# An fp32 encoder layer on one core: the key transpose on VectorE, the scores' diagonal by a column sum, and other moves around TensorE

## What is computed

```python
forget = lb + (1.0 - lb) * jax.nn.sigmoid(ff)
k = (1.0 - lb) * jax.nn.sigmoid(-ff)
# per chunk, G the running sum of log(forget)
A = jnp.einsum('bhid,bhijd,bhjd->bhij', q, decay, k)      # j <= i
o = einsum('bhij,bhje->bhie', A, v) + einsum('bhid,bhde->bhie', q * exp(G), state)
state = exp(G_last) * state + einsum('bhjd,bhje->bhde', k * exp(G_last - G), v)
o = _rmsnorm(o, norm_g) * jax.nn.silu(og)
```

## Time and profile before

| what | value |
|---|---|
| median of 3 runs | 2827.2 us (2826.24 to 2828.23) |
| the profiled execution | 2829.01 us, its span 2827.2 us |
| PE busy | 2813.3 us, 100% of the span |
| VectorE, ScalarE, GpSimd busy | 1539.8, 734.1, 123.9 us |
| mean granted clock | 0.998 |
| HBM traffic | 217 GB/s over the span |

### The profile page before, as it was taken

How to read it: one execution, slowest core, us unless ns; L and a number is a source line. 1 busy time by engine, 2 the same in 40 slices (tenths; PEclk the granted TensorE clock), 3 DMA queues, 4 the chain that set the end, 5 groups by cost and what they waited for, 6 DMA issues and landing times.

```text
span 2827.2 us, 32881 instructions
## 1 busy us (share of the span) xinstructions
PE 2813.3 (100%) x12966; PEld 2349.1 (83%) x12966; DVE 1539.8 (54%) x3012; ACT 734.1 (26%) x1005; POOL 123.9 (4%) x72
## 2 busy tenths in 40 slices
PE   9999999999999999999999999999999999999998
PEld 7888888888888888888888888888888888888887
DVE  6895777756377345553347734555334772555521
ACT  5333344433122113221112211222111220222200
POOL 1003400024000000000000000000000000000000
PEclk9999999999999999999999999999999999999999
DMA  8668988888744565556564455555656445555555
GB/s 305 232 239 271 313 283 289 292 321 317 247 149 164 178 216 190 194 193 235 208 224 148 159 197 210 194 194 193 230 213 214 154 148 212 203 193 193 194 208 177
DMA packets 123738, 614.57 MB, mean 217 GB/s; under 512 B 13987, under 2 KB 16337, under 8 KB 76096
## 3 DMA queue, kind: packets, MB, share of 16 engines
q1 hardware_dynamic: 122544, 610.39, 61.1%
q0 software_dynamic: 896, 1.97, 0.2%
q10 hardware_dynamic: 144, 0.11, 0.0%
HBM read 474.00 MB, written 138.41 MB: 217 GB/s over the span
## 4 chain that ended last, share of the span: by engine, by line
PE 97%; DVE 1%; DMA 1%; issue 0%; ACT 0%; POOL 0%; SPq 0%; POOLq 0%; DVEq 0%; ACTq 0%
PE bank L1182 28%; PE bank L1183 28%; PE bank L1189 28%; PE bank L1247 2%; PE bank L1249 2%; PE bank L1248 2%; PE bank L1262 2%; PE bank L1357 1%; DMA w_split<-w_both 1%; PE bank L1384 1%; PE bank L1389 1%; PE bank L1380 1%; PE bank L1375 0%; PE bank L1198 0%; PE bank L1195 0%; PE bank L1196 0%
## 5 line engine op out<-in xcount | busy, mean ns | idle before, releaser
L1182 PE MATMUL bank<-h_hi,w_both 128*128 128x512 f32 x2400 | 939.3, 391 | 0.0
L1183 PE MATMUL bank<-h_lo,w_both 128*128 128x512 f32 x2400 | 934.4, 389 | 0.0
L1189 PE MATMUL bank<-h_hi,w_both 128*128 128x512 f32 x2400 | 593.4, 389 | 0.0
L1189 PEld LDWEIGHTS bank<-h_hi,w_both 128*128 128x128 f32 x2400 | 450.5, 188 | 93.5
L1183 PEld LDWEIGHTS bank<-h_lo,w_both 128*128 128x128 f32 x2400 | 450.7, 188 | 92.5
L1182 PEld LDWEIGHTS bank<-h_hi,w_both 128*128 128x128 f32 x2400 | 450.7, 188 | 92.5
L1072 DVE TENSOR_TENSOR z<-bank,rms_inv 128x512 f32<-128x512 f32 x176 | 121.8, 692 | 341.2 <-PE bank L1189 340.8
L1085 DVE SCALAR_TENSOR_TENSOR conv<-z,params,conv 128x512 f32<-128x512 f32 x352 | 263.6, 750 | 6.5 <-DVE halo L1075 0.3
L1183 PE MATMUL bank<-g_lo,w_both 128*128 128x512 f32 x682 | 265.3, 389 | 0.0
L1182 PE MATMUL bank<-g_hi,w_both 128*128 128x512 f32 x682 | 265.3, 389 | 0.0
L495 ACT ACTIVATE w_both<-raw 128x1024 fp32r<-128x1024 f32 x122 | 129.4, 1060 | 341.7 <-PE bank L1189 296.9
(11 more groups left out here) (267 smaller groups left out, 3151.1 us busy)
## 6 DMA issues: line engine op xcount, KB each, us to landing
w_both<-w_split SPq DMA_DIRECT2D x371, 1024.0 KB, 4.8
w_split<-w_both SPq DMA_DIRECT2D x248, 512.0 KB, 5.7
raw<-w_units SPq DMA_DIRECT2D x123, 512.0 KB, 5.3
x_in<-x_t SPq DMA_DIRECT2D x32, 256.0 KB, 5.7
res<-x_t SPq DMA_DIRECT2D x32, 256.0 KB, 5.2
out<-res SPq DMA_DIRECT2D x24, 256.0 KB, 7.1
out<-res SPq DMA_DIRECT2D x16, 128.0 KB, 1.9
w_both<-w_split SPq DMA_DIRECT2D x2, 512.0 KB, 6.9
```

Of the source, the lines that this page charges most:

```text
L1182: pe.matmul(dst, w_hi[slot][:, off + k, :], rhs_hi(k), start=first and k == 0, stop=False)
L1183: pe.matmul(dst, w_hi[slot][:, off + k, :], rhs_lo(k), start=False, stop=False)
L1189: mm = pe.matmul(dst, w_lo[slot][:, off + k, :], rhs_hi(k), start=False, stop=last and k == n - 1)
```

## The change

- `s1` is now level 1 as the other levels are (two fp32 matmuls of 128 columns, into bank 3) and the diagonal apart: VectorE forms qk = q0 * kp, ScalarE its upper half, VectorE the rest, and PE sums both over the channels with two fp32r matmuls of 512 columns against ones (bank 4). Mask 0 picks the diagonal. The keys of all levels are now made in place in `kp`.
- In tiles 1 to 3 the keys are transposed by VectorE, in 16 pieces of 32 partitions by 4 x 32, between the queries and the masks. Tile 0 keeps PE's transposes.
- forget and k (two instructions each), `a_hi` and `b_hi` go from VectorE to ScalarE; `b_hi` and `b_lo` of a head are made within the next head.
- `v_head` moves from before the masks to behind them.
- The fifth of a head's six `w_lo` pieces of tile 0 moves behind the state update.
- The six sum matmuls move into the fourth unit, behind its first eight matmuls.
- The parameters go to the front of SyncE's queue. SyncE waits, before it loads unit 1 of tile 1, until both halves of unit 0 have landed.

```diff
-    level_place = {64: (5, 0), 32: (5, 1), 16: (6, 0), 8: (6, 1), 4: (7, 0), 2: (7, 1)}
+    level_place = {64: (5, 0), 32: (5, 1), 16: (6, 0), 8: (6, 1), 4: (7, 0), 2: (7, 1), 1: (3, 0)}
...
+            if g == 1:
+                sp.wait_ge(both_in[slot_of(1, 0)], 32)
...
+        sp.dma_start(params[:, :], par).then_inc(par_in, 16)
         load_x(0, 0)
         load_raw(0)
...
-        act.dma_start(params[:, :], par).then_inc(par_in, 16)
...
+            def b_upper(h):
+                act.wait_ge(*head_dve.at("b", t * NH + h))
+                act.activation(b_hi[:, h, :], og_act[:, :], ACT.Copy).then_inc(*b_act.did("b_hi"))
...
                 act.activation(sig_nf[:, :], bank[0][:, :], ACT.Sigmoid, scale=-1.0).then_inc(evac[0], 1)
+                for dst, src in zip(parities(total[1][:, :]), by_parity(sig_f[:, :])):
+                    op = act.activation(dst, src, ACT.Identity, bias=lower[:, 2, bass.ds(h, 1)], scale=keep)
+                op.then_inc(*head_act.did("forget"))
+                act.wait_ge(evac[0], t * B_TILE + h * 3 + B_HEAD + 1)
+                for dst, src in zip(parities(kp[:, :]), by_parity(sig_nf[:, :])):
+                    op = act.activation(dst, src, ACT.Copy, scale=keep)
+                op.then_inc(*head_act.did("k"))
+                if h:
+                    b_upper(h - 1)
                 unit_behind(t, U_HEAD + 1, u)
                 act.activation(sig_q[:, :], bank[1][:, :], ACT.Sigmoid).then_inc(*head_act.did("sig_q"))
+                act.wait_ge(*head_dve.at("qk", it))
+                act.activation(qk_hi[:, :], qk[:, :], ACT.Copy).then_inc(*head_act.did("qk_hi"))
...
+                act.wait_ge(*head_dve.at("a", it))
+                act.activation(a_hi[:, h, :], gm_mix[:, :], ACT.Copy).then_inc(*head_act.did("a_hi"))
+            b_upper(NH - 1)
...
+                dve.tensor_tensor(qk[:, :], q0[:, :], kp[:, :], ALU.mult).then_inc(*head_dve.did("qk"))
+                dve.tensor_tensor(qp[:, :], q0[:, :], total[1][:, :], ALU.mult).then_inc(*head_dve.did("qp1"))
...
                 weights_lo(t, next_lo + 1)
+                if h:
+                    b_lower(h - 1)
...
+                    if s == 16:
+                        dve.wait_ge(*head_act.at("qk_hi", it))
+                        dve.tensor_tensor(qk_lo[:, :], qk[:, :], qk_hi[:, :].bitcast(F32),
+                                          ALU.subtract).then_inc(*head_dve.did("qk_lo"))
...
+                if t:
+                    then(f"kl{P}")
+                    for a in range(0, P, 32):
+                        for b in range(0, P, 32):
+                            op = dve.transpose(blocks(k_tok[b:b + 32, :], P)[:, :, a:a + 32], blocks(kp[a:a + 32, :], P)[:, :, b:b + 32])
+                    op.then_inc(*keys_dve.did("k_tok"))
...
                 dve.tensor_copy(state[:, 0, :], carry[:, h, :]).then_inc(*head_dve.did("st0"))
-                weights_lo(t, next_lo + 4)
+                dve.wait_ge(*ln_dve.at("inv", t))
+                for c in range(NC):
+                    dve.tensor_scalar(v_head[:, c * P:(c + 1) * P], v_tok[:, c, bass.ts(h, P)], moments[:, c, 0:1],
+                                      spreads[:, 1, c:c + 1], ALU.subtract, ALU.mult).then_inc(*head_dve.did(f"vh{c}"))
                 dve.wait_ge(*head_pe.at("update", it))
...
+                weights_lo(t, next_lo + 4)
                 dve.wait_ge(*head_pe.at("mix", it))
...
                 dve.wait_ge(*head_act.at("o_rms", it))
                 dve.reciprocal(head_o[:, :], head_o[:, :]).then_inc(*head_dve.did("inv"))
+                dve.wait_ge(*head_act.at("a_hi", it))
+                dve.tensor_tensor(a_lo[:, h, :], gm_mix[:, :], a_hi[:, h, :].bitcast(F32),
+                                  ALU.subtract).then_inc(*head_dve.did("a_lo"))
...
+                    if n == 3 and k == 2 * n4 and not lower:
+                        first_sums()
...
-                for c in range(NC):
-                    mm = pe.matmul(first[:, c // 2, c % 2, :], kp[:, c * P:(c + 1) * P], q_both[:, c, :],
-                                   start=True, stop=True)
-                mm.then_inc(*head_pe.did("s1"))
+                level(1)
+                pe.wait_ge(*head_act.at("qk_hi", it))
+                pe.matmul(bank[4][:, :], ones_r[:, :], qk_hi[:, :], start=True, stop=False)
+                pe.wait_ge(*head_dve.at("qk_lo", it))
+                pe.matmul(bank[4][:, :], ones_r[:, :], qk_lo[:, :], start=False, stop=True).then_inc(*head_pe.did("s1"))
                 from_h(t, U_HEAD + 4, u, 0, used + 2)
-                pe.wait_ge(*head_dve.at(f"kl{P}", it))
-                flip(bank[2], k_all, NC - (t == NT - 1)).then_inc(*head_pe.did("k_tok"))
+                if t == 0:
+                    pe.wait_ge(*head_dve.at(f"kl{P}", it))
+                    flip(bank[2], kp, NC).then_inc(*keys_pe.did("flip"))
```

More of the change, by code:

```diff
@@ L249, in build @@
     lnb_row, bs_row = temp("lnb_row", 0), temp("bs_row", 2)
[L251 to L256, removed]
+    bank = [nc.alloc_psum_tensor(f"bank{i}", [P, TT], F32) for i in range(8)]
     def sem(name):
@@ L277, in build @@
     tok_act = Steps(sem("tok_act"), ["v0", "v1"] + [f"i{c}" for c in range(NC)])
[L278 to L280 removed]
+    head_act = Steps(sem("head_act"), ["i_head", "sig_f", "forget", "k", "sig_q", "qk_hi", "sig_og", "o_sq", "sq_hi", "o_rms", "a_hi"])
+    head_pe = Steps(sem("head_pe"), ["s1", "s2_4", "s8_16", "s32_64", "update", "o", "mix", "o_sum"])
+    names = ["floor", "qk", "qp1", "qr1"]
     for s in LEVELS:
[L282 removed]
+        names += (["qk_lo"] if s == 16 else []) + [f"kc{s}", f"kl{2 * s}", f"t{2 * s}"]
     for s in LEVELS:
         names += ([f"qr{s}"] if s > 1 else []) + [f"qp{2 * s}"]
[L285 to L287 removed]
+    head_dve = Steps(sem("head_dve"), names
+                     + ["m1", "m0", "m2", "m4", "m8", "m16", "m32", "m64", "st0"] + [f"vh{c}" for c in range(NC)] + ["st1", "st2", "st3", "st4",
+                        "mix", "sq_lo", "a", "inv", "a_lo", "unit", "b"])
+    b_act, b_dve = Steps(sem("b_act"), ["b_hi"]), Steps(sem("b_dve"), ["b_lo"])
+    keys_pe, keys_act = Steps(sem("keys_pe"), ["flip"]), Steps(sem("keys_act"), ["k_tok"])
+    keys_dve = Steps(sem("keys_dve"), ["k_tok"])
     ln_dve = Steps(sem("ln_dve"), [f"bn{c}" for c in range(NC)] + [f"ag{c}" for c in range(NC)] + ["inv"])
@@ L875, in then @@
                     dve.wait_ge(*head_dve.at(name, it))
[L877 to L885, removed]
+                dve.wait_ge(*head_act.at("forget", it))
                 dve.tensor_scalar(total[1][:, :], total[1][:, :], TINY, None, ALU.max).then_inc(*head_dve.did("floor"))
@@ L1008, in _ @@
                 op.then_inc(*head_dve.did("b"))
[L1009 to L1013 removed]
+            b_lower(NH - 1)
             dve.wait_ge(evac[0], t * B_TILE + B_MIX)
@@ L1263, in level, with first_sums @@
             return mm
+        def first_sums():
+            pe.wait_ge(*pre_dve.at("sum", KD - 1))
+            token_sums(bank[5], sum_n)
+            pe.wait_ge(sums_back, 1)
+            for c in range(NC // 2):
+                mm = pe.matmul(bank[5][:, NC + c:NC + c + 1], sum_r[:, c * P:(c + 1) * P], ones[:, 0:1],
+                               start=True, stop=True)
+            mm.then_inc(first_ssq, 1)
         def for_first_tokens(n, dst, is_v):
```

100 lines of the change are left out of this document (34 added, 66 removed).

## The result

The changed kernel takes **2836.72 us** in the median of 7 runs (2836.18 to 2838.08), against 2827.2 of the kernel before on the same chip: ratio 1.0033, 95% interval 1.0023 to 1.0043. It is 9.5 us slower, where 2813.5 was forecast and a chance of 0.05 given to slower. The profiled execution took 2836.18 us, its span 2834.4.

What follows compares the result with a forecast made beforehand. PE, busy all of the span, was taken as the bound. Gains of 17.0 less losses of 3.4, 13.6 net, took the profiled 2829.0 to 2815.4, or 2813.5 us in the median; range 2810.3 to 2821.5, with 0.58 on 2810.3 to 2816.

Steps and rivals of the forecast that it cites:

- Does VectorE deliver in tiles 1 to 3?: Prediction's step on whether VectorE, transposing keys in tiles 1 to 3, finishes the last mask before PE asks: cost 0.
- 16 t: Time of a head's sixteen VectorE transposes, t each; up to 3.4 us, t up to 0.21, was to cost nothing.
- A wait at the update in each head of tiles 1 to 3: Sign against the forecast: PE waiting at the state update, by 16 (t - 0.21) in each head.
- `s1`, transposes off PE: PE work removed: cheaper s1 in 16 heads, 6.3 us gained; 44 key transposes in tiles 1 to 3, 4.8 us gained.
- tile 0's heads: PE waits in tile 0's heads 1 to 3 as VectorE runs later, 0.9 each: cost 2.7 us, bounds 0 and 6.
- halves of a and b, DMA: Longer chain to b_lo at a tile's end, cost 0.2 us; raw units landing late at the denser start, cost 0.5.
- start: Sums inside the fourth unit remove PE's idle time and the clock stays high: gain 4.4 us, about 1.5 if it falls.
- hold at unit 1: SyncE holds the load of unit 1 of tile 1, so unit 0 lands sooner: gain 1.5 us, bounds 0 and 1.5.
- Rival 3: VectorE becomes the bound of tiles 1 to 3 at 0.37 us a transpose: 29 us lost, 2842; chance 0.05.
- Rival 1: The clock falls anyway at the start: 2816.5 us; chance 0.14.

## Why the prediction was wrong

**The step that failed** is the price in "Does VectorE deliver in tiles 1 to 3?": "I take 0.21, since the pieces depend on nothing among themselves and have no pointers". They do depend on nothing, and 0.21 is what such pieces take in the mean while they stay in one quarter. But each piece of a real transpose changes the quarter that it reads or writes, and then waits for the end of the one ahead: 0.32. A price near it was at hand: "a dependent small instruction, some 0.37" (in the state's updates of the kernel before, L975, three take 842.39 - 841.25 = 1.14), which I kept as an end of the range without a reason why a piece could be held like one.

**What stood around it was right.** The chain was to end 21.10 us + 16 t after the queries' start; with t = 0.323 that is 26.27, and 26.24 was measured. "16 t may be 3.4": in tile 1, head 1 the update is 1.76 late, and 5.17 - 1.76 = 3.4. That the first head of each tile pays 0.6 less came out in tiles 2 and 3 (waits of 1.01 for 1.59), not in tile 1 (1.35). The consequence was named too: "A wait at the update in each head of tiles 1 to 3 would make the forecast wrong". What I did wrong with it was the odds. A forecast that stands exactly on the edge of its slack, with one price unmeasured, is not worth 0.58; every error upward costs twelve heads, and none downward gives anything.

**What spoke against it** had the price. The Trainium skill, "VectorE: DVE Perf Modes", has in its table of the three transpose paths 311 ns for a 128 x 128 tile of bf16, where a piece here lasts 303 ns, and its rule gives the transpose to TensorE. Worked out as the price of each piece, that gave about 2831, an estimate. My ground for setting it aside, that the figure is of a single instruction, was an assumption: the table does not say so, and whether one piece overlaps the next is what its section on held instructions, named above, is about.

**Term by term**, from the forecast to the result:

| term | forecast | found | from |
|---|---|---|---|
| `s1`, transposes off PE | -6.3, -4.8 | as forecast | period 40.41 with one transpose |
| transposes by VectorE | 0 | +20.6 (spans), +21.2 (times) | one transpose in place of 16 |
| tile 0's heads | +2.7 | +3.3 | below |
| halves of a and b, DMA | +0.7 | about 0 | no row of a wait |
| start | -4.4 | -4.9 profiled, -3.3 in medians | start as before |
| hold at unit 1 | -1.5 | -0.6 to -1.0 | hold taken out |

With the medians' start that is 2827.2 - 11.1 + 21.2 + 3.3 - 3.3 - 1.0 = 2836.3, or 2835.7 with 20.6; 2836.7 was measured. The start's 4.9 is of one pair of profiles: PE's first `back_hi` matmul comes at 36.90 and 37.09 in the kernel before and at 31.99 in the changed one, but between 32.44 and 33.47 in the ten other kernels with that start, which is 3.4 to 4.7 earlier.

Tile 0: PE's way to the FFN's first sum was 361.54 - 36.90 = 324.64 before, less four times 0.39 should be 323.08, and was 326.36: 3.3 lost. The wait for `qk_lo` came where it was forecast, three times; the list gives 0.2, but from start to start it is 118.00 - 117.33 = 0.67 in place of 0.31, the 0.4 of the forecast. In head 1 the level matmuls take 0.3 more, paced by VectorE's queries (3.14 for 24 records where the earlier trace rows has 2.84). The update costs another 0.3: it starts 132.87 - 130.88 = 1.99 after the matmuls ahead of it, 1.81 before, and takes 0.99 in place of 0.89. Head 0, which the prediction had free, pays the last two as well.

**The rivals.** Rival 3, the one on the slower side, is what happened, at the value where it "turns to slower by over 0.2%", t = 0.32. By its own formula it gives 2832.8 at that price; the 3.9 us from there to the result lie in the loss beyond each wait, the first head of tile 1, the start, the hold and tile 0. Its condition, a piece as slow as a dependent small instruction, was right in kind, and "no piece waits on another", the ground for its 0.05, was what failed. Rival 1 did not come: the clock stayed up in every kernel with the sums in the fourth unit. But I counted the gain from an execution that had the low clock for all of the stretch, and took its 1.8 us over the median for noise that moves the whole sum. Part of it may be this very term; no profile of the kernel before with the clock up is there to show it.

## To carry to other kernels

Price a run of small VectorE instructions by whether each is held by the one ahead: at 128 elements a change of partition quarter made it 0.32 us where free ones went at 0.21, and an instruction that needs the result ahead is held alike (a copy of 256 elements, 0.32 in place of 0.20). When work goes from the bounding engine to one with idle time, write down that engine's chain between two dates of the bound one and ask for more slack than the dearest plausible price, or shorten the chain first: here moving instructions into an idle stretch and interleaving two dependent loops turned a loss of 9.5 us into a gain of 14.3 (2826.9 to 2812.5). And a term read off one execution should be checked against what differs between executions.

## What was not expected of the hardware

- VectorE's transpose costs by the instruction, 0.30 us for 32 x 128 and for 64 x 128, 0.71 for 128 x 512: by these two sizes about 0.17 + 0.00105 an element, an estimate. Sixteen pieces cost eight times what one whole instruction does.
- A key product of 256 elements lets an independent instruction start after 0.34 us and the copy that needs its result after 0.53; a copy 0.20 and 0.32. Interleaving two such chains took a level of each from 0.86 + 0.79 to 1.07 us.
- A wait costs PE some 0.25 us more than the idle time that is listed: 20.6 us lost for 17.7 of waits. 0.17 of it is the listed length of the matmuls ahead, which overlaps with what follows when nothing is late, and 0.10 is the slower update. Short delays of the update are not listed at all: 0.3 in the kernel with pieces in their own quarter, 0.2 in tile 0 of the changed kernel.
- Behind an idle time of 1.28 to 1.87 us and the sums, the granted clock of the next 5.3 us was 0.50, 0.50, 0.68 and 1.00 in four profiled executions of three kernels. No kernel was profiled with both outcomes.
